# Two transformer layers in one kernel: where the block norms' last residuals and panel splits stand, and a distance table written in six transfers instead of two

## What is computed

```python
def hybrid_layer(x, c, ...):
    shift, scale, gate = split(silu(c) @ w_ada + b_ada, 3)
    h = rms_norm(x, norm_gain) * (1 + scale) + shift            # norm_a
    q_a, k_a, v_a, z_a, q_b, kc, vc, ks, vs, kw, vw, z_b, g_b = split(h @ w_in)
    o_a = banded_gqa(qa, ka, v_a, 128, rel_bias[:, :8], sinks)  # bias = rel_bias[t5_bucket(t - s)]
    k_cmp, v_cmp = compress_blocks(kc, ...), compress_blocks(vc, ...)
    o_b = gated sum of nsa_cmp_sel(...) and banded_gqa(qb, k_win, vw, 512, rel_bias[:, 8:])
    return x + gate * (concat(o_a * silu(z_a), o_b * silu(z_b)) @ w_out)

# then, with mod = silu(c) @ ada_w + ada_b for each of two layers:
h = rmsnorm(x, norm1[0]) ...;  x = x + gate * diff_attention(h, ctx)       # norm_b
h = rmsnorm(x, norm2[0]) ...;  x = x + gate * swiglu(h, gate_up, down)     # norm_d
h = rmsnorm(x, norm1[1]) ...;  x = x + gate * short_conv(h, ...)           # norm_e
h = rmsnorm(x, norm2[1]) ...;  x = x + gate * swiglu(h, gate_up, down)     # norm_f
```

## Time and profile before

| what | value |
|---|---|
| runs before, median (lowest to highest of 3) | 1718.24 us (1718.07 to 1719.33) |
| profiled execution, its own time | 1718.99 us |
| its span | 1717.2 us, 22981 instructions |
| mean granted TensorE clock | 0.997 |
| TensorE matmul busy | 1671.4 us, 97% |
| TensorE weight load busy | 1383.1 us, 81% |
| VectorE, ScalarE, GpSimd busy | 57%, 40%, 4% |
| DMA | 202.02 MB, mean 118 GB/s |
| chain that ended last | PE 86%, DVE 7%, DMA 3%, ACT 2% |

### The profile page before, as it was taken

The page is one execution under the profiler, slowest core; times in us unless marked ns, Lnnn a source line. Parts: engine busy times, 40 slices in busy tenths (PEclk is TensorE's granted clock), DMA queues, the critical chain, the costliest instruction groups (busy, mean ns, idle before and its releaser), DMA issues.

```text
span 1717.2 us, 22981 instructions
## 1 busy us (share of the span) xinstructions
PE 1671.4 (97%) x8926; PEld 1383.1 (81%) x8926; DVE 976.0 (57%) x1806; ACT 678.5 (40%) x1413; POOL 61.8 (4%) x120
## 2 busy tenths in 40 slices
PE   6999999999999999999999999999999999999998
PEld 3677777788999999777888888887888788888887
DVE  5667567857677667766555554336565633333332
ACT  3434556654355545644232323223222422333221
POOL 0000000000000000000000000000000000000000
PEclk9999999999999999999999999999999999999999
DMA  8886333303213222223666665443433233333332
GB/s 309 228 249 188 92 98 112 87 19 86 62 50 111 50 86 73 64 62 90 187 190 190 176 176 143 118 117 86 135 110 103 81 98 98 98 95 95 96 114 80
DMA packets 290215, 202.02 MB, mean 118 GB/s; under 512 B 76247, under 2 KB 272072, under 8 KB 289082
## 3 DMA queue, kind: packets, MB, share of 16 engines
q1 hardware_dynamic: 266942, 133.21, 27.9%
q0 software_dynamic: 15536, 56.37, 10.9%
q10 hardware_dynamic: 7628, 10.97, 1.9%
HBM read 197.33 MB, written 5.28 MB: 118 GB/s over the span
## 4 chain that ended last, share of the span: by engine, by line
PE 86%; DVE 7%; DMA 3%; ACT 2%; issue 2%; SPq 1%; DVEq 0%; ACTq 0%
PE PS L869 13%; PE PS L871 13%; PE PS L870 13%; PE PS L851 5%; PE PS L852 5%; PE PS L853 5%; PE PS L1293 3%; PE PS L1295 3%; PE PS L1294 3%; PE PS L1343 3%; PE PS L1102 2%; PE PS L1367 2%; PE PS L1076 1%; PE PS L1355 1%; PE PS L903 1%
## 5 line engine op out<-in xcount | busy, mean ns | idle before, releaser
L2032 DVE TENSOR_TENSOR WL<-WS,WH 128x512 fp32r<-128x512 f32 x416 | 268.3, 687 | 247.1 <-ACT WH L1520 246.8
L1520 ACT ACTIVATE WH<-WS 128x512 fp32r<-128x512 f32 x416 | 237.9, 621 | 179.8 <-PE PS L853 135.0
L869 PE MATMUL PS<-A3H,WL 128*128 128x512 f32 x672 | 262.8, 391 | 0.1
L871 PE MATMUL PS<-A3H,WH 128*128 128x512 f32 x672 | 261.6, 389 | 0.0
L870 PE MATMUL PS<-A3L,WH 128*128 128x512 f32 x672 | 261.4, 389 | 0.0
L869 PEld LDWEIGHTS PS<-A3H,WL 128*128 128x128 f32 x672 | 126.1, 188 | 30.3 <-issue 4.5
L871 PEld LDWEIGHTS PS<-A3H,WH 128*128 128x128 f32 x672 | 126.1, 188 | 26.3
L870 PEld LDWEIGHTS PS<-A3L,WH 128*128 128x128 f32 x672 | 126.2, 188 | 25.8
L851 PE MATMUL PS<-GH,WL 128*128 128x512 f32 x352 | 137.4, 390 | 0.6 <-DVE WL L2032 0.6
L853 PE MATMUL PS<-GH,WH 128*128 128x512 f32 x352 | 137.0, 389 | 0.0
L852 PE MATMUL PS<-GL,WH 128*128 128x512 f32 x352 | 137.0, 389 | 0.0
(11 more groups left out here) (361 smaller groups left out, 3422.9 us busy)
## 6 DMA issues: line engine op xcount, KB each, us to landing
AW<-in_ada_w POOLq DMA_DIRECT2D x96, 512.0 KB, 4.2
WS<-in_ffn_w_gate_up SPq DMA_DIRECT2D x88, 512.0 KB, 4.5
WS<-in_ffn_w_down SPq DMA_DIRECT2D x32, 512.0 KB, 4.2
WS<-in_sc_w_in SPq DMA_DIRECT2D x24, 512.0 KB, 4.0
AB<-in_w_ada SPq DMA_DIRECT2D x8, 1024.0 KB, 15.8
WS<-in_w_in SPq DMA_DIRECT2D x32, 256.0 KB, 4.9
WS<-in_diff_w_qkv SPq DMA_DIRECT2D x64, 128.0 KB, 2.6
WS<-in_ffn_w_down SPq DMA_DIRECT2D x16, 384.0 KB, 3.5
```

Source lines behind the costliest of these rows:

```text
L869: mm(PS[:, b, :], wl[:, k, :], hi[:, k, 0:S], start=(k == 0), stop=False)
L871: m = mm(PS[:, b, :], wh[:, k, :], hi[:, k, 0:S], start=False, stop=(k == KT - 1))
L1520: f(weights(p)[0][:, k, :], WS[:, p % 2, k, :], ACT.Copy).then_inc(w_hi, 1)
L2032: tt(lo[:, k, :], WS[:, p % 2, k, :], hi[:, k, :].bitcast(F32), ALU.subtract).then_inc(w_lo, 1)
```

## The change

There are five edits.

1. norm_b: VectorE does `second_residual(7)` ahead of `add_squares(6, 14)` rather than behind it.
2. norm_b: `fill(2)` no longer waits for `ln_lo` 16 at its head; inside its first half it waits for `ln_lo` 8 + k + 1 ahead of slice k, eight waits.
3. norm_d, norm_e, norm_f: the split of the pair's second panel (two copies on ScalarE, two subtractions on VectorE) moves ahead of the last residual: for up0 into the loop over the eight residual tiles at t = 6, for conv_in and up1 into `residual_tile` of the last pass, tile 1.
4. down0: `add_pieces` moves from behind the second residual tile of a pass to between the first and the second.
5. The distance table: the two transfers inside norm_a's `layer_norm` go. Instead ScalarE issues six in stage z, one in each of t = 1 to 6, behind the split of panel t + 1 and ahead of the hidden part's split: two of 4 heads by 128 rows of 1 KB, four of 2 heads by 128 rows of 2 KB, 512 KB each. The wait ahead of `TBA` becomes 16 x 6.

```diff
--- before.py
+++ after.py
@@ -1274,8 +1274,6 @@
                 if n < 2:
                     pe.wait_ge(ctx_lo, 4)
                     pe.wait_ge(out_res, 3 + n)
-                if n == 2:
-                    pe.wait_ge(ln_lo, 16)
                 if n == 4:
                     pe.wait_ge(ln_lo, 24)
                 for m in range(n - 1, -1, -1):
@@ -1288,6 +1286,8 @@
                     tok = slice((2 * (a % 2) + half) * P, (2 * (a % 2) + half + 1) * P)
                     o = out[:, 2 * P * half:2 * P * (half + 1)]
                     for k in range(KT):
+                        if n == 2 and half == 0:
+                            pe.wait_ge(ln_lo, 8 + k + 1)
                         wh, wl = weights(p + k // 4)
                         wh, wl = slab(wh, k % 4), slab(wl, k % 4)
                         mm(o, th[:, k, tok], wl, start=(k == 0), stop=False)
@@ -1559,20 +1559,20 @@
                 if 0 in tiles:
                     root(At(stage), 0, RS[:, 0, 0:n], 1.0 / D, ln_rs, n)
                 if first_panels is not None:
-                    send_distances()
                     for j in range(2):
                         split(first_panels, j)
                 for k in tiles:
                     act.wait_ge(ln_t, 8 * L + k + 1)
                     f(dst[:, k, tok], RAW[:, k % 2, 0:n], ACT.Identity, bias=bias[:, k:k + 1]).then_inc(ln_hi, 1)
 
-            def send_distances():
-
-                act.wait_ge(rows_out, 16)
-                for head, at, n in ((0, 3 * P - 1, 2 * P), (8, P - 1, S)):
-                    act.dma_start(dist_table[head:head + 8, :, 0:n],
-                                  bass.AP(dist_rows.tensor, head * 640 + at, [[640, 8], [-1, P], [1, n]]))\
-                        .then_inc(dist_out, 16)
+            def send_distances(q):
+
+                if q == 0:
+                    act.wait_ge(rows_out, 16)
+                head, heads, at, n = (4 * q, 4, 3 * P - 1, 2 * P) if q < 2 else (4 + 2 * q, 2, P - 1, S)
+                act.dma_start(dist_table[head:head + heads, :, 0:n],
+                              bass.AP(dist_rows.tensor, head * 640 + at, [[640, heads], [-1, P], [1, n]]))\
+                    .then_inc(dist_out, 16)
 
             act.dma_start(XS[:, :, :], ins["x"][0].rearrange("(t p) d -> p t d", p=P)).then_inc(x_in, 16)
             act.wait_ge(vec_zero, 1)
@@ -1637,6 +1637,8 @@
             for t in range(8):
                 if t:
                     split(a, t + 1)
+                if 1 <= t <= 6:
+                    send_distances(t - 1)
                 if t >= HIDDEN_AT:
                     split_hidden(t - HIDDEN_AT)
                 if t == 7:
@@ -1679,7 +1681,7 @@
             load_set(LN_AND_EXP)
             act.wait_ge(gate_in, 1)
             f(GT[:, :, :], GT[:, :, :], ACT.Exp, scale=-1.0).then_inc(gate_exp, 1)
-            act.wait_ge(dist_out, 32)
+            act.wait_ge(dist_out, 16 * 6)
             act.dma_start(TBA[:, :, 0:2 * P], dist_table[0:8, :, 0:2 * P].rearrange("h p n -> p h n")).then_inc(table_a, 16)
             head_root(a, 0, 0)
             for j in range(4):
@@ -1826,6 +1828,8 @@
             def residual_tile(a, t, per, r, more=True, squared=True):
                 for p in range(per):
                     split(a, per * t + p + 1, more or t == 0 or p < per - 1)
+                if squared and a.i == 3 and t == 1:
+                    split_panel(a.panel(2 * per) + 1)
                 if squared:
                     squares(a, t, 2 * a.i + (8 * r + t), one(H, a.i, 2, t))
 
@@ -1972,12 +1976,13 @@
                 for hd in heads_at(t):
                     split_head(hd)
             for t in range(8):
+                if t == 6:
+                    split(At("up0"), 1)
                 act.wait_ge(wo_res, 8 + t + 1)
                 act.wait_ge(ss_add, 14 + t)
                 f(SQ[:, t % 2, :], H[:, t, :], ACT.Square).then_inc(h_sq, 1)
 
             def ffn(l, stage, L, shift, r, squared):
-                split(At(f"up{l}"), 1)
                 split(At(f"up{l}"), 2)
                 layer_norm(stage, L, A3H, slice(0, S), M2[:, shift:shift + 8])
                 load_set(SILU)
@@ -1995,7 +2000,6 @@
                 residual(f"down{l}", r, squared)
 
             ffn(0, "norm_d", 3, 24, 3, True)
-            split(At("conv_in"), 1)
             split(At("conv_in"), 2)
             layer_norm("norm_e", 4, A4H, slice(0, S), M2[:, 48:56])
             for a, _ in passes(act, "conv_in"):
@@ -2498,11 +2504,11 @@
                 for a, more in passes(dve, stage):
                     for t in range(2):
                         residual_tile(a, t, a.pg // 2, r, gate, more, squared)
+                        if stage == "down0" and t == 0:
+                            add_pieces(92 + a.i, 93 + a.i)
                         if stage == "down1" and a.i and t == 0:
                             take_out(2 * a.i - 2)
                             take_out(2 * a.i - 1)
-                    if stage == "down0":
-                        add_pieces(92 + a.i, 93 + a.i)
 
             def take_layer_part(stage, u, n, bank=None):
 
@@ -2557,8 +2563,8 @@
             split_panel(P_DIFF + 1)
             add_squares(5, 13)
             second_residual(6)
+            second_residual(7)
             add_squares(6, 14)
-            second_residual(7)
             add_squares(7, 15)
             for q in range(2, 4):
                 split_panel(P_DIFF + q)
```

## The result

The changed kernel takes 1755.76 us in the median of 4 runs (1754.84 to 1756.39), against 1718.55 for the kernel before beside it. The ratio is 1.0212, with a 95% interval of 1.0199 to 1.0225, so it is slower by 37 us. The profiled execution took 1756.39 us with a span of 1754.6, 37.4 longer than before.

What follows compares the result with a forecast made beforehand. TensorE was taken to bound the kernel. From 1719.0 profiled, pieces +37 (34 + 7 - 4.2) and norms -4.5 gave 1751.5, or 1750.8 in the median: 1751. The forecast's own range was 1733 to 1775, the overall range 1714 to 1776.

Steps and rivals of the forecast that it cites:

- pieces on few engines: Stage z: each table piece uses only as many engines as heads outermost, four or two; 1751 us, chance 0.68.
- z's start: Ahead of z: without the table the first panel lands earlier, TensorE idles 0.8 instead of 3.34, clock holds; -4.2 us.
- The pieces in z: Stage z: panels wait behind table pieces on the busiest engines; +34 us for 2 KB pieces, +7 for 1 KB ones.
- One for one: Stage z: on a shared engine one panel packet passes per table packet, so a panel behind the table takes 13.2 us.
- the other loads: Stage z: modulation and compression weights queue on the busiest engine too, 1.5 to 3 us more per 2 KB step.
- Where TensorE waits: Stage z: TensorE would wait for the vector split of the weights, some 8 us per panel.
- ScalarE held at issue: Rival, stage z: a piece's issue waits for an earlier one to drain, 2 to 4 us each; around 1770, chance 0.08.
- Spread wide: Rival, stage z: each piece uses eight engines whatever its heads, 1 us on each of six steps; 1715.5, chance 0.12.
- The norms: norm_b, norm_d, norm_e, norm_f: reordered residual, tile-wise wait and moved splits together give -4.5 us, bounds -1.5 and -7.
- the lower bound: norm_b: the tile-wise wait gains 0 of the 1.1 us taken, since the turn and fill behind wait for vector work.
- The wait for the table: At TBA's load: it moves with the stage and stays covered, the last piece ending near 145 us.

Runs made afterwards that it cites:

- e2: Changed kernel with its six pieces laid with 128 rows outermost instead of heads, row step +1 instead of -1; ratio 1.0001 to the kernel before.
- e1: Changed kernel with the table's two transfers put back into norm_a, so only the norm edits are left; 1715.62 us, ratio 0.9977 to the kernel before.
- e8: Changed kernel with six eight-head pieces issued in norm_a's layer norm behind ScalarE's tiles 3 to 8; 1720.46 us, ratio 1.0012 to the kernel before.
- e6: Changed kernel with the table as one 4 MB transfer, 16 heads outermost, at its old place in norm_a; 1715.44 us, ratio 0.9985 to the kernel before.

## Why the prediction was right, and where its steps were not

The forecast was 1751, the measured time 1755.8, inside its own range. The mechanism, pieces on few engines, is the one that the runs show. That the sum came so near is in part luck, as the second step says. By its steps; z's start is measured at its tenth product, at full clock in both, 64.23 us before and 59.46 after:

- **z's start.** Forecast -4.2, measured -4.8. Without the table the panels ahead of z land 4.1 us after their issue (the median from 34 to 58 us), before the layer norm ends, TensorE doesn't wait at all where 0.8 was forecast, and the clock holds at 1.00 from 60 to 65 us.
- **The pieces in z.** Forecast +41, measured 41.3 + 4.8 = +46. One for one on two engines is right: 43 packets beside 42 on 1.8 engines, 0.049 us for the 1 KB packet against the 0.048 taken. The landings of 12.9 us are near the 13.2 worked out, but like the 12.7 of the earlier trace rows they are those of half a panel with its other half in the queue; the whole panel in the chain took 14.94. The term was mis-sized because it left out the clock: TensorE's waits grew by only 35 us (35.7 and 0.6 now, 1.3 before), and the other 11 have no wait of TensorE's to their name. They are the 22.55 us of work at 0.50, half of which full speed would have saved; the step time of TensorE, 7.1, was taken at full speed. So the waits were put 6 us too high and the clock's 11 us at nothing, and the two errors partly cancel. The 1.5 to 3 us a step for the other loads came from no row, and no run separates them.
- **Where TensorE waits.** The forecast named the vector split of z's panels, 8 us for each. It is wrong: that split ends 0.6 us of waiting, and the hidden part's 35.7, and not in equal steps: 7.74 and 17.98 for the first two, 10 for the other three. The panels have two slots, the compression's weights one, and they stand behind the panels in SP's queue: 19.58 us, of which only part is their own, since from its issue to 99.8 us that queue moves nothing but packets under 512 bytes, the panels'. This was in the rows: TensorE's waits in z before were for the hidden part.
- **ScalarE held at issue.** This rival is out: 0.58 to 0.70 us per piece. It is SP that is held, 2.73 and 6.98 us in the chain.
- **Spread wide.** It is what e2 shows, with a size too small: I put 6 us on six steps, it costs 9. A row at 1.18 of the engines says that there is no room; what in the 7.1 worked out for a step was too small, the runs don't separate.
- **The norms.** Forecast -4.5, measured -4.0 (e1) and -3.9 (the two traces). norm_d and norm_e are as worked out: `RAW` waits for `RS` there. norm_e's wait fell to 1.3, not to 0.9, and (1 - 0.67) x 5 = 1.6 us of lowered clock went: 0.9 + 1.6 = 2.5. The starts of the same TensorE products in the two traces bear this out: they lie 41.3 us apart ahead of norm_b, 40.3 behind it, 39.9 behind norm_d, 37.5 behind norm_e and 37.4 at the end. So norm_e gave 2.4, norm_d 0.4 or 0.5, norm_f 0.1, as forecast. norm_b gave 1.0, where 1.4 was forecast: its fill starts earlier at a full clock, and gives most of that back by the turn (L1321), the way that the lower bound had feared.
- **The wait for the table** stayed covered: `TBA` is loaded 41.3 us later because the stage is that much later, none of its packets is left after 147.1 us, near the 145 worked out, and nothing in TensorE's waits names the table.

## What to carry to other kernels

Give a transfer from DRAM to DRAM a large count outermost: cutting this one along its heads made pieces that were each as long as a whole transfer and all on the same engines, and cost 45 us, where the same bytes with 128 rows outermost cost 9. Ask of a moved transfer what its busiest engine carries in the new place, and add the lowered clock behind each wait that it makes. Look for a place where the DMA share is low rather than one where the compute engine is busy, and for what the transfer still reaches into: e8 began at a share of 0.00, and TensorE then waited 7.5 us for the next panel.

## What the runs showed that was not expected

That two busy engines hold up a load on all sixteen was forecast; that the wait would be for the block behind the panels was not. This 512 KB block of the compression's weights took 19.58 us while the share fell to 0.44, and TensorE waited for it and hardly for the panels. A quarter of what z lost, 11 of 46 us, is the lowered clock, which no wait names. And putting the table on all sixteen engines is no gain in itself: in e6 it only hands the wait from z's first panel to kcvc's second.
